# Seven block products in place of eight in the second block's feed-forwards of a one-core kernel

## The reference, cut to what matters

```python
D_MODEL, SEQ, CTX_LEN, D_FF_2 = 1024, 256, 256, 2816

def swiglu(h, w_gate, w_up, w_down):
    return (jax.nn.silu(h @ w_gate) * (h @ w_up)) @ w_down

for i in range(DEPTH):
    ...
    x = x + g1 * y
    x = x + g2 * swiglu(modulate(x, norm_ffn_g[i], sh2, sc2),
                        ffn_w_gate[i], ffn_w_up[i], ffn_w_down[i])
    if not last:
        ctx = ctx + cg1 * yc
        ctx = ctx + cg2 * swiglu(modulate(ctx, norm_ffn_g[i], csh2, csc2),
                                 ffn_w_gate[i], ffn_w_up[i], ffn_w_down[i])
return rmsnorm(x, final_norm_g)
```

## Time and profile before

| | us |
|---|---|
| median of 3 runs (2909.4 to 2914.75) | 2911.96 |
| the profiled execution | 2908.36 |
| its span, first to last instruction | 2906.3 |
| gate and up of layer 0, TensorE | 303.0 |
| down of layer 0, TensorE | 151.35 |
| gate and up of layer 1, TensorE | 153.9 |

### The profile page before, as it was taken

How to read it: one execution, slowest core, us unless ns; L and a number is a source line. 1 busy time by engine, 2 the same in 40 slices (tenths; PEclk the granted TensorE clock), 3 DMA queues, 4 the chain that set the end, 5 groups by cost and what they waited for, 6 DMA issues and landing times. The chain is left out here.

```text
span 2906.3 us, 33918 instructions
## 1 busy us (share of the span) xinstructions
PE 2736.0 (94%) x14316; PEld 1832.6 (63%) x14316; DVE 1159.2 (40%) x2257; ACT 500.8 (17%) x1151; POOL 246.7 (8%) x292
## 2 busy tenths in 40 slices
PE   5999999899899999989979999999999899999998
PEld 4778886774577888677445554444444466665873
DVE  1355434966325543493421642000000358961001
ACT  1241210100025121010011531000000333421000
POOL 1001210110000121011000000000000025520000
PEclk9989999999999999989999999999999999999999
DMA  6322114777433211477742002222222254334442
GB/s 213 101 95 89 31 45 145 226 252 244 161 109 100 90 31 45 145 225 241 259 142 72 1 6 66 74 72 75 85 67 67 75 159 129 117 102 128 155 148 99
DMA packets 276941, 340.42 MB, mean 117 GB/s; under 512 B 7188, under 2 KB 227348, under 8 KB 276664
## 3 DMA queue, kind: packets, MB, share of 16 engines
q1 hardware_dynamic: 264880, 309.61, 33.4%
q10 hardware_dynamic: 8760, 17.64, 1.8%
q0 software_dynamic: 3152, 11.01, 1.1%
HBM read 337.05 MB, written 1.19 MB: 116 GB/s over the span
## 5 line engine op out<-in xcount | busy, mean ns | idle before, releaser
L383 PE MATMUL PS<-MEM 128*128 128x512 f32 x1424 | 614.5, 593 | 8.8 <-POOL MEM L2181 2.4
L855 PE MATMUL PS<-MEM 128*128 128x512 f32 (+2 forms) x1840 | 616.5, 496 | 4.6 <-ACT MEM L1269 4.6
L855 PEld LDWEIGHTS PS<-MEM 128*128 128x128 f32 (+1 forms) x1840 | 347.3, 189 | 270.0 <-issue 241.5
L383 PEld LDWEIGHTS PS<-MEM 128*128 128x128 f32 x1424 | 269.5, 190 | 349.4 <-issue 334.7
L1064 ACT ACTIVATE MEM<-PS 128x256 f32<-128x256 f32 (+4 forms) x459 | 196.4, 442 | 1521.5 <-PE PS L855 478.6
L354 PE MATMUL PS<-MEM 128*128 128x256 f32 x1760 | 401.3, 390 | 9.8 <-DMA MEM<-w_up 8.1
L354 PEld LDWEIGHTS PS<-MEM 128*128 128x128 f32 x1760 | 343.6, 197 | 63.7 <-DMA MEM<-w_up 11.2
L1528 DVE SCALAR_TENSOR_TENSOR MEM<-MEM 128x256 f32<-128x256 f32 x560 | 264.9, 506 | 12.0
L1921 DVE TENSOR_TENSOR MEM<-PS,MEM 128x512 f32<-128x512 f32 (+1 forms) x44 | 24.6, 559 | 433.6 <-PE PS L855 433.6
L560 PE MATMUL PS<-MEM 128*128 128x256 f32 x768 | 172.3, 382 | 0.0
L961 PE MATMUL PS<-MEM 128*128 128x512 f32 (+1 forms) x512 | 171.2, 487 | 0.0
(11 more groups left out here) (301 smaller groups left out, 2425.9 us busy)
## 6 DMA issues: line engine op xcount, KB each, us to landing
MEM<-w_in SPq DMA_DIRECT2D x54, 1024.0 KB, 5.4
MEM<-ada_w SPq DMA_DIRECT2D x48, 1024.0 KB, 5.4
MEM<-w_up SPq DMA_DIRECT2D x32, 1024.0 KB, 6.3
MEM<-w_down SPq DMA_DIRECT2D x32, 1024.0 KB, 5.1
MEM<-ssm_w_in SPq DMA_DIRECT2D x24, 1024.0 KB, 5.5
MEM<-ffn_gate SPq DMA_DIRECT2D x22, 1024.0 KB, 5.3
MEM<-ffn_up SPq DMA_DIRECT2D x22, 1024.0 KB, 5.3
MEM<-ffn_down SPq DMA_DIRECT2D x20, 1024.0 KB, 5.0
```

The source lines that it names most:

```text
L383: ins = pe.matmul(banks[t], src(kk, t), W[:, k, :], start=kk == 0, stop=kk == nk - 1)
L855: ins = pe.matmul(bank[0:m, 0:hi - lo], W[:, k, c * P:c * P + m], XT2[:, k, lo:hi], start=k == 0, stop=k == KT - 1)
```

## The change

Gate and up (all slabs but gate's first one in each layer) and, in layer 0, the down product are computed by blocks: both operands are cut in 2 by 2 blocks, and seven products of sums of blocks take the place of eight products of blocks; the results are put together from the seven by additions. In gate and up a block of the weights is 512 channels by 128 columns and a block of the input 512 channels by half of the tokens: 256 in layer 0, where each half is a stream, and 128 in layer 1. In down a block of the hidden values is a stream by every second hidden block, and a block of the weights 256 columns. VectorE makes the sums of the token blocks once (XSUM), the sums of the weight blocks for each slab (WSUM, DSUM) and of the hidden blocks (HSUM), and the additions behind; ScalarE copies the first product (E1, D1) and applies Silu to a slab of gate in memory. TensorE takes four banks for a slab of gate or up and seven for a half of down. TM2 moves to another address. The diff, cut:

```diff
-            def feed_forward(l, streams):
...
-                for s in range(NF2 // 2):
-                    channels2(io["ffn_gate"][l], 256 * s, 256, [("fg", l, 2 * s), ("fg", l, 2 * s + 1)], ("act",) * 2, 0, streams * T)
-                    channels2(io["ffn_up"][l], 256 * s, 256, [("fu", l, 2 * s), ("fu", l, 2 * s + 1)], ("dve",) * 2, 0, streams * T)
-                emptied(pe, ("fu", l, NF2 - 1))
-                wide(io["ffn_down"][l], lambda k, t: HID2[:, k, t * P:(t + 1) * P], NF2, lambda h, t: ("fd", l, h, t), nt=NT * streams)
+        DOWN7 = [(half, max(0, k0), 4 if k0 > 0 else 2) for half in range(2) for k0 in range(-2, NF2, 4)]
+        DOWN_BANKS = ("p1", "p6", "p2", "p7", "p5", "p4", "p3")
+        SEVENS = [(l, kind, s) for l in range(2) for s in range(NF2 // 2) for kind in ("fg", "fu") if s or kind == "fu"]
...
+            def seven_products(w, l, kind, s):
...
+                b = take((l, kind, "b", s), "dve")
...
+                product(a[:, x], W[:, lo, m0], XT2[:, lo, x]).then_inc(S("seven_part"), 1)
+                pe.wait_ge(S("w_summed"), n + 1)
+                if (kind, s) == ("fu", 0):
+                    pe.wait_ge(S("x_summed"), l + 1)
+                done(product(b[:, x], sums(1), XSUM[:, 1, :, x]))
+                product(c[:, x], sums(2), XSUM[:, 2, :, x]).then_inc(S("seven_part"), 1)
+                product(d[:, x], sums(0), XSUM[:, 0, :, x]).then_inc(S("seven_part"), 1)
+                pe.wait_ge(S("p1_copied"), n + 1)
+                done(product(a[:, y], W[:, hi, m0], XT2[:, hi, x]))
+                pe.wait_ge(S("u_summed"), 2 * n + 1)
+                done(product(c[:, y], W[:, hi, m1], XSUM[:, 3, :, x]))
+                pe.wait_ge(S("u_summed"), 2 * n + 2)
+                done(product(d[:, y], sums(3), XT2[:, hi, y]))
+                close_slab()
+            def down_sevens(w):
...
+                    if k0 == 0:
+                        banks = {name: take((name, half), "act" if name == "p1" else "dve") for name in DOWN_BANKS}
+                    pe.wait_ge(S("hid2_done"), (k0 + n) // 2)
+                    for name in DOWN_BANKS:
+                        if name == "p6":
+                            pe.wait_ge(S("down_summed"), i + 1)
...
+                                ins = pe.matmul(banks[name][:, t * T:(t + 1) * T], left[:, t * P:(t + 1) * P], right,
+                                                start=f == 0 and t == 0, stop=f == NF2 // 2 - 1 and t == NT - 1)
...
+            def feed_forward_sevens(l):
...
+                channels2(io["ffn_gate"][l], 0, 256, [("fg", l, 0), ("fg", l, 1)], ("act",) * 2, 0, (2 - l) * T)
+                for m, kind, s in SEVENS:
+                    if m == l:
+                        seven_products(io["ffn_gate" if kind == "fg" else "ffn_up"][l], l, kind, s)
+                if l == 0:
+                    down_sevens(io["ffn_down"][l])
+                else:
+                    pe.wait_ge(S("hid2_done"), NF2)
+                    wide(io["ffn_down"][l], lambda k, t: HID2[:, k, t * P:(t + 1) * P], NF2, lambda h, t: ("fd", l, h, t))
...
         @block.scalar
...
+                def p1(i):
...
+                    act.activation(E1[:, i % 2, 0:tn], bank_of((l, kind, "a", s))[:, 0:tn], ACT.Copy).then_inc(S("p1_copied"), 1)
...
+                        h = HID2[:, 2 * s:2 * s + 2, 0:2 * tn]
+                        act.activation(h, h, ACT.Silu).then_inc(S("gate_silu"), 1)
...
         @block.vector
...
+                dve.tensor_tensor(q(2), b22, b12, ALU.subtract)
+                link(dve.tensor_tensor(q(0), b12, b11, ALU.subtract))
+                link(dve.tensor_tensor(q(1), b22, q(0), ALU.subtract))
+                dve.tensor_tensor(q(3), b21, q(1), ALU.subtract).then_inc(S("x_summed"), 1)
+                def weights(i):
...
+                    dve.wait_ge(S(f"slab_loaded{at % NSLOT}"), 16 * (at // NSLOT + 1))
...
+                    dve.tensor_tensor(q(2), a11, a21, ALU.subtract)
+                    link(dve.tensor_tensor(q(0), a21, a22, ALU.add))
+                    link(dve.tensor_tensor(q(1), q(0), a11, ALU.subtract))
+                    dve.tensor_tensor(q(3), a12, q(1), ALU.subtract).then_inc(S("w_summed"), 1)
...
+                    b = filled(dve, "dve", (l, kind, "b", s))
+                    dve.wait_ge(S("p1_copied"), i + 1)
+                    read(dve.tensor_tensor(U2[:, 0:tn], b[:, 0:tn], E1[:, i % 2, 0:tn], ALU.add))
+                    settle()
+                    dve.wait_ge(S("seven_part"), 3 * i + 2)
+                    dve.tensor_tensor(U3[:, 0:tn], bank_of((l, kind, "c", s))[:, 0:tn], U2[:, 0:tn], ALU.add).then_inc(S("u_summed"), 1)
+                    dve.wait_ge(S("u_summed"), 2 * i + 1)
+                    dve.wait_ge(S("seven_part"), 3 * i + 3)
+                    dve.tensor_tensor(c22, bank_of((l, kind, "d", s))[:, 0:tn], U3[:, 0:tn], ALU.add)
+                    dve.tensor_tensor(U4[:, 0:tn], bank_of((l, kind, "d", s))[:, 0:tn], U2[:, 0:tn], ALU.add).then_inc(S("u_summed"), 1)
+                    if i + 1 in mine:
+                        weights(i + 1)
+                    elif l == 0:
+                        down_weights(0)
+                    b = filled(dve, "dve", (l, kind, "a", s))
+                    read(dve.tensor_tensor(c11, b[:, tn:2 * tn], E1[:, i % 2, 0:tn], ALU.add))
...
+                        dve.tensor_tensor(h4, h4, UPR[:, :, 0:tn].rearrange("p (a b) n -> p a b n", a=2), ALU.mult).then_inc(S("hid2_multiplied"), 1)
...
+            def down_joined(n):
...
+                        b = bank("p4", half)
+                        link(added(DA2, 1, cb))
+                        read(dve.tensor_tensor(DA1, b, D3, ALU.add))
+                        settle()
+                        link(scaled(DA1, 1, ca))
+                        b = bank("p3", half)
+                        read(dve.tensor_tensor(DA2, b, D4, ALU.add))
+                        added(DA1, 1, ca)
+                        settle()
+                        link(scaled(DA2, 0, cb))
+                        ins = added(DA2, 0, cb)
...
+                    if i + 2 < len(DOWN7):
+                        down_weights(i + 2)
```

More of the change, by code:

```diff
@@ L857, in channels2, with product @@
                 close_slab()
-            def feed_forward(l, streams):
-                n = 2 * l + 1
-                gate_rows(n, l, 5, streams)
-                turn_normed(n, streams)
-                for s in range(NF2 // 2):
-                    channels2(io["ffn_gate"][l], 256 * s, 256, [("fg", l, 2 * s), ("fg", l, 2 * s + 1)], ("act",) * 2, 0, streams * T)
-                    channels2(io["ffn_up"][l], 256 * s, 256, [("fu", l, 2 * s), ("fu", l, 2 * s + 1)], ("dve",) * 2, 0, streams * T)
-                emptied(pe, ("fu", l, NF2 - 1))
-                wide(io["ffn_down"][l], lambda k, t: HID2[:, k, t * P:(t + 1) * P], NF2, lambda h, t: ("fd", l, h, t), nt=NT * streams)
+            def seven_products(w, l, kind, s):
+                n = len(seven_at)
+                assert SEVENS[n] == (l, kind, s)
+                tn = P if l else T
+                W = a_slab(w, 256 * s)
+                seven_at.append(len(slabs) - 1)
+                b = take((l, kind, "b", s), "dve")
+                a = take((l, kind, "a", s), "dve")
+                c = take((l, kind, "c", s), "dve")
+                d = take((l, kind, "d", s), "dve")
+                x, y = slice(0, tn), slice(tn, 2 * tn)
+                lo, hi, m0, m1 = slice(0, 4), slice(4, 8), slice(0, P), slice(P, 2 * P)
+                sums = lambda i: WSUM[:, n % 2, i, :, :]
+                def product(out, left, right):
+                    for k in range(4):
+                        ins = pe.matmul(out, left[:, k, :], right[:, k, :], start=k == 0, stop=k == 3)
+                    return ins
+                product(a[:, x], W[:, lo, m0], XT2[:, lo, x]).then_inc(S("seven_part"), 1)
[12 more added lines that the diff above has]
+                close_slab()
@@ L1271, in modulated, with feed_forward_sevens @@
                         ins.then_inc(S("bank_read_by_act"), 1)
-            def feed_forward(l, streams):
+            def feed_forward_sevens(l):
                 n = 2 * l + 1
[L1275 to L1279, removed]
+                tn = P if l else T
+                squares2(n, NT * (2 - l))
+                gate_rows(n, 2 - l)
+                modulated(n, 2 - l)
+                for f in range(2):
+                    copy(("fg", l, f), HID2[:, f, 0:2 * tn], lambda b: b[:, 0:2 * tn], ACT.Silu)
+                first = l * len(SEVENS) // 2
+                mine = range(first, first + len(SEVENS) // 2)
+                def p1(i):
+                    act.wait_ge(S("seven_part"), 3 * i + 1)
+                    _, kind, s = SEVENS[i]
+                    if i >= 2:
+                        emptied(act, SEVENS[i - 2][:2] + ("a",) + SEVENS[i - 2][2:])
```

(32 more changed lines are left out.)

145 lines of the change are left out of this document (130 added, 15 removed).

## The result

The changed kernel takes 2842.9 us (median of 4 runs, 2841.4 to 2847.6) against 2910.7 us (4 runs): a ratio of 0.977, 95% interval 0.9752 to 0.9788, faster by 67.8 us. 2850 was forecast, with a range of 2842 to 2874, so the result lies at the range's lower end.

A forecast was written before the change was run, and what follows sets the result against it. TensorE's record spacing was taken to bound both feed-forwards, other engines almost idle. 67.0 + 0.8 - 0.3 - 2.0 - 0.8 - 4 = 60.7 us gained: 2847.7 from the profiled run, 2851.3 from the median; forecast 2850, range 2842 to 2874.

The forecast's parts named there:

- layer 0, gate and up, with the wait that goes: First feed-forward: 21 slabs at 12.09 us instead of 13.77, 35.3 us gained; TensorE's wait before down goes, 0.8 us gained.
- layer 0, down, with the 0.3 between the halves: Layer 0's down: 616 records, 133.0 us, for 352, 151.35 us: 18.3 gained; waiting for banks between halves loses 0.3.
- tail behind layer 0's down: After layer 0's down, p4's VectorE chain runs into p3's, 3.5 us, and ScalarE's squares wait: 2.0 us lost.
- layer 1, gate and up, records alone: Last feed-forward: 56 records at 0.112 us per slab, 6.27 us for 6.91, over 21 slabs: 13.4 us gained.
- layer 1, switch to down: Last layer's switch to down: c12 and the product come behind the last matmul instead of one operation: 0.8 us lost.
- layer 1, hand-over: VectorE's loop per layer 1 slab, 6.3 us against TensorE's 6.27: extra waits taken as 0.2 per slab, 4 us lost.
- rival 2: Waits reach layer 0 too, or sums run slower beside other engines: 0.5 us in 42 slabs, about 2870; chance 0.07.
- rival 1: VectorE's hand-over sets layer 1's period at 7.0 us, so its gate and up gain nothing: 2857 to 2860; chance 0.16.
- The term of 0.15 us for TensorE to start again: Layer 1's loop: after the weight sums, TensorE needs 0.1 to 0.2 us to start again, taken as 0.15.
- VectorE's share in layer 1: VectorE was to be busy over 80% in layer 1's gate and up, a sign of the forecast.
- Rival 3: 128-column matmuls held by exposed weight loads, 0.190 us a record: 27 us slower, 2937; chance 0.03.
- Rival 4: Small gaps in the last layer keep the clock at 1.2 GHz, 128 columns taking twice as long: some 2960; chance 0.02.

The follow-up runs named there:

- the run with the needless operation: Changed kernel plus an unneeded 512-element VectorE operation ahead of each of 20 weight sums of layer 1, between U4 and the sums: 2853.5 us.
- down_both: Changed kernel with layer 1's down product by seven products too, token halves of 128: 2838.0 us, ratio 0.9754.
- down_both_ctx_early: Seven products in both layers' down, first weight sum ahead of c22, ScalarE squaring the context's tiles before x's: 2834.9 us; run again, 2833.5 us.
- down_old: Changed kernel with layer 0's down product put back as before, gate and up by sevens: 2860.1 us, ratio 0.9833.
- l0_old: Changed kernel with layer 0's gate and up put back as before, down by sevens: 2879.0 us, ratio 0.9896.

## Why the prediction was right

By its steps (us gained; seams with a minus where they cost):

| step | forecast | measured |
|---|---|---|
| layer 0, gate and up, with the wait that goes | 35.3 + 0.8 | 35.5 |
| layer 0, down, with the 0.3 between the halves | 18.3 - 0.3 | 17.3 |
| tail behind layer 0's down | -2.0 | -2.05 |
| layer 1, gate and up, records alone | 13.4 | 13.8 |
| layer 1, switch to down | -0.8 | -0.65 |
| layer 1, hand-over | -4 | 0 |
| between the two feed-forwards | 0 | 0.2 |
| stages ahead | 0 | 1.5 |
| sum | 60.7 | 65.6 |

- **The rates.** Spacings of 0.216 and 0.112 us were forecast and 0.2164 and 0.1118 came. The 0.0005 us a record between 0.2164 and the rate used (12.09 / 56) make up the 0.6 us that layer 0's gate and up fell short, and 0.3 of the 0.7 in down; another 0.2 there is the end of the last old record, which the forecast's 151.35 us contain.
- **Layer 0.** TensorE waited for VectorE in none of the 21 slabs (no spacing over 0.220 us); rival 2 fell. VectorE was busy 55%, 6.6 us of a slab of 12.1; "8 to 9" was right for up slabs alone.
- **The tail.** The forecast named p4's chain that runs into p3's. VectorE ends 3.5 us behind the last matmul as it said, and the run with the old down has the 6.83 us back.
- **The mis-sized term** is "I take 0.2 per slab, 4 us lost" for layer 1's hand-over. The loop was forecast at 6.3 us and is 6.25; TensorE's slab is 6.26. So the loss is zero, but by a hundredth of a microsecond, and rival 1, which had 0.16, was one operation away: 0.12 us more in the loop already costs 2.5 us. The forecast had no row for the extra waits and took 0.2 for them; in the lines above they cost no time of the loop. VectorE's operations with a wait for a bank ahead of them (L2081, L2083, L2086) start 0.20 us apart, as c22 and U4 do that have none between them. The term of 0.15 us for TensorE to start again was right: where it had to wait, in the run with the needless operation, its first matmul started 0.06 us behind the last sum and the second came 0.10 late.
- **Layer 1's records.** The 0.4 us over the forecast are less than what the clock can do there: the unchanged first gate slab ran at a granted clock of 0.81 (0.80 in the kernel before) and took 8.55 us, and 6.98 us at 1.00 in the second run of the changed kernel. That both kernels had it low in the profiled execution is luck; otherwise this row would differ by 1.6 us.

```profile
2610.63:2619.18 8.55, 8.55 (x32) 7.25 (x33) 5.27 (x8) 0.76 (x2) 0.00 (x0) 0.81 0.01 2
2609.47:2616.45 6.98, 6.98 (x32) 6.11 (x33) 5.27 (x8) 0.76 (x2) 0.00 (x0) 1.00 0.00 0
```

- **VectorE's share in layer 1** was forecast at over 80% and is 72%: results not linked to each other start 0.2 us apart, where I had added up durations.
- **Rival 3** (bare weight loads, 0.190 a record) is refuted by layer 1's spacing: loads of 0.192 us every 0.112 us. The Trainium skill's rule that loads overlap running matmuls only when their row groups differ (TensorE: Matmul & The Clock Gate, "The mechanism") does not hold here; the measured stage decides. The same page puts a load at its columns over 1.2 GHz ("LDWEIGHTS (loading the stationary operand)"), by which 128 columns would take an estimated 107 ns. The run with 64 moving columns comes near that as a pace, 112 ns a record, and disagrees with it as a duration, 192 ns.
- **Rival 4** fell too: the granted clock was 1.00 in both stages of sevens.

The total came 7.1 us below 2850. Of this 4 are the mis-sized term and 1.5 the stages ahead, which is luck; 2.3 are what the forecast had put on top of its 2847.7 for the median of the kernel before; the small rows take 0.6 back. The range's lower end, 2842, was meant for no loss in the last layer and a good run, and that is what came.

## What to carry to other kernels

Where TensorE sets the pace and VectorE stands idle beside it, seven block products in place of eight are worth their eighth of the records, fp32 records of 256 columns being half as long as those of 512; below 128 columns nothing is left behind 128x128 weights, because their loads take over at 0.112 us. Write the hand-over as a loop (last product, first result, sums, next product) and compare its length with TensorE's slab: only operations inside it count, and a few lines of order decide whether one costs 0.6 us or nothing. Where such a loop is full, the first thing to move is a sum that depends on no product, into a wait for one.

## What the runs showed of the hardware that was not expected

- Weight loads of 128x128 fp32 overlap each other as well as the matmuls: their records last 0.192 us and come every 0.112 us, and PEld is busy 130.00 of 130 us. Loads of 128x64 come every 0.055 us.
- The spread between executions lies mostly outside the changed stages. Gate and up of layer 0 began anywhere from 1794.3 to 1801.3 us in kernels that are alike up to there (both ends are down_both and down_both_ctx_early). In these two the granted clock over the whole run, 0.967 and 0.964, goes with it, but not in all: the runs with 0.968 began at 1794.28 (down_old) as well as at 1798.15 (the kernel before). Why was not looked into. The seven-product records of layer 1 repeat to some hundredths of a microsecond (131.48 to 131.52 us; 131.67 in l0_old, where one slab waited 0.19), while the old gate slab ahead of them takes 6.98 to 8.98 us with the clock. For a difference of a few microseconds the length of such a group of records tells more than the run's time.
